# Retention transposes of a gMLP and retention layer moved from TensorE to transposing DMAs, with the scores four steps behind

## What is computed

```python
q = rotary(r_q...); k = rotary(r_k...)            # 128 per head; v has 256 per head
scores = einsum('bnthd,bnshd->bnhts', q, k) * decay     # inside a chunk
inner  = einsum('bnhts,bnshe->bnthe', scores, v)
kv     = einsum('bnshd,bnshe->bnhde', k * w_state, v)   # what a chunk adds to the state
cross  = einsum('bnthd,bnhde->bnthe', q, r_prev) * cross_decay   # r_prev: state before the chunk
ret    = standardize(inner + cross)                     # per head
yb     = (ret * silu(r_z)) @ w_ob
```

## Time and profile before

| | |
|---|---|
| median of 3 runs | 2732.95 us (2732.89 to 2733.12) |
| the profiled execution | 2732.09 us, span 2730.5 us |
| spans of the cores | 2728.6 to 2730.5 us (even), 2684.2 to 2694.5 us (odd) |
| busy on the slowest core (core 2) | PE 2697.4 us (99%), DVE 1108.5 us (41%), ACT 643.5 us (24%) |
| table loads of ACT | 34, 1283 ns each |
| share of the 16 DMA engines | POOL's queue 41.3%, SP's queue 4.6% |

### The profile page before, as it was taken

The page is one execution under the profiler, slowest core; times in us unless marked ns, Lnnn a source line. Parts: engine busy times, 40 slices in busy tenths (PEclk is TensorE's granted clock), DMA queues, the critical chain, the costliest instruction groups (busy, mean ns, idle before and its releaser), DMA issues.

```text
span 2730.5 us, 42159 instructions; the slowest of 8 cores (2684.2 to 2730.5 us)
## 1 busy us (share of the span) xinstructions
PE 2697.4 (99%) x15129; PEld 1420.4 (52%) x15170; DVE 1108.5 (41%) x2686; ACT 643.5 (24%) x1546; POOL 194.5 (7%) x370
## 2 busy tenths in 40 slices
PE   8999999999999999999999999999999999999998
PEld 6556666555555666666544444444555444444443
DVE  1444441166664422222474343411666642122157
ACT  1221110155554111111001211111555621111100
POOL 2000000000000000000001000000000000000000
PEclk9999999999999999999999999999999999999999
DMA  9843444333225433344649464444333544444443
GB/s 159 175 78 63 69 74 71 60 63 58 47 53 109 70 73 68 69 70 70 143 174 214 81 93 72 73 87 76 63 63 63 108 78 89 74 70 86 77 122 134
DMA packets 62420, 241.54 MB, mean 88 GB/s; under 512 B 7424, under 2 KB 7552, under 8 KB 58624
## 3 DMA queue, kind: packets, MB, share of 16 engines
q0 software_dynamic: 52560, 193.49, 41.3%
q1 hardware_dynamic: 9648, 45.27, 4.6%
HBM read 413.31 MB, written 18.87 MB: 158 GB/s over the span
## 4 chain that ended last, share of the span: by engine, by line
PE 97%; DMA 1%; ACT 1%; issue 0%; DVE 0%; POOL 0%; POOLq 0%; DVEq 0%; ACTq 0%
PE ps_all L236 96%; PE ps_all L245 1%; DMA ring<-w 1%; ACT L257 0%; DVE xy_85 L264 0%; ACT aT L257 0%; POOL xT L292 0%; POOL ring L292 0%; POOLq L988 0%; ACT zth_124 L257 0%; DVE stv L282 0%; ACT rs_66 L257 0%; ACT rs_63 L257 0%; ACT rs_65 L257 0%; ACT zth_123 L257 0%
## 5 line engine op out<-in xcount | busy, mean ns | idle before, releaser
L236 PE MATMUL ps_all<-xT,ring 128*128 128x384 bf16 (+1 forms) x6400 | 1206.6, 348 | 0.8 <-ACT rs_65 L257 0.7
L236 PEld LDWEIGHTS ps_all<-xT,ring 128*128 128x128 bf16 x6400 | 622.1, 98 | 536.6 <-issue 2.4
L236 PE MATMUL ps_all<-ring,xT 128*128 128x512 bf16 (+1 forms) x3744 | 731.1, 353 | 5.1 <-DMA xT<-xT 3.1
L236 PEld LDWEIGHTS ps_all<-ring,xT 128*128 128x128 bf16 x3744 | 337.4, 98 | 341.1 <-issue 6.9
L236 PE MATMUL ps_all<-aT,ring 128*128 128x384 bf16 (+1 forms) x2520 | 481.2, 347 | 2.1
L236 PEld LDWEIGHTS ps_all<-aT,ring 128*128 128x128 bf16 x2560 | 250.2, 98 | 220.0
L292 POOL DMA_DIRECT2D ring<-w x352 | 187.7, 541 | 2409.9 <-PE ps_all L236 2013.4
L236 PE MATMUL ps_all<-ring,yT 128*128 128x512 bf16 x1088 | 235.2, 379 | 0.0
L236 PEld LDWEIGHTS ps_all<-ring,yT 128*128 128x128 bf16 x1088 | 106.4, 98 | 128.4
L275 DVE CAST yT<-ps_all 128x384 bf16<-128x384 f32 (+1 forms) x40 | 24.5, 611 | 205.7 <-PE ps_all L236 205.7
L264 DVE SCALAR_TENSOR_TENSOR ogb_129<-ogb_129,ps_all 128x384 f32<-128x384 f32 (+1 forms) x40 | 24.3, 608 | 183.6 <-PE ps_all L236 183.6
(11 more groups left out here) (271 smaller groups left out, 1895.4 us busy)
## 6 DMA issues: line engine op xcount, KB each, us to landing
ring<-w POOLq DMA_DIRECT2D x352, 512.0 KB, 6.3
xy_86<-x SPq DMA_DIRECT2D x9, 1024.0 KB, 6.8
out<-xy_86 SPq DMA_DIRECT2D x18, 512.0 KB, 3.1
xy_85<-x SPq DMA_DIRECT2D x8, 1024.0 KB, 5.4
out<-xy_85 SPq DMA_DIRECT2D x16, 512.0 KB, 2.6
xT<-xT POOLq DMA_DIRECT2D x9, 512.0 KB, 26.3
xT<-xT POOLq DMA_DIRECT2D x4, 1024.0 KB, 21.3
bias_71<-bias_s SPq DMA_DIRECT2D x2, 1024.0 KB, 12.2
```

The source lines that it names most:

```text
L236: return self.S.op("pe", lambda e: e.matmul(out, lhsT=l, rhs=r, start=start, stop=stop), [l, r], [out])
```

## The change

```diff
 def rotary(i):
     ...
+    self.dma_tr("tq%d" % (i % 6), m.qkT[i % 6][:], o[:].rearrange("p j f -> p (j f)"))

 def small_pe(i):
-    a, b_, c_, y = i - 2, i - 3, i - 4, i - 7
-    if 0 <= a < N:
-        for j in range(2):
-            self.tr(self.bank16(3)..., m.qkt[a % 6][:, j, :])
+    b_, c_ = i - 4, i - 5
     ...
-    if 0 <= y < N:
-        for j in range(2):
-            self.tr(self.bank16(7)..., m.ybp[y % 4]...)

 def small_post(i):
     ...
-    if 0 <= a < N:
-        self.act(m.qkT[a % 4]..., self.bank16(3)[:, 0:256], AF.Copy)
     ...
     if 0 <= z < N:          # z = i - 6, before i - 5
         self.act(m.ybp[z % 4][:], self.bank(5 + z % 2)[:, 0:256], AF.Identity, ...)
-    if 0 <= y < N:
-        self.act(self.aT[...], self.bank16(7)..., AF.Copy)
+        self.dma_tr("ty%d" % (z % 4), self.aT[:, 2 * h:2 * h + 2, c * 128:(c + 1) * 128], m.ybp[z % 4][:])
```

The ring is refilled differently during the retention: not four units when a head's last group has been recorded, but one in every other step, behind that step's group:

```diff
-    if c == n - 1:
-        self.w_free()
+    if c % 2 == 0:
+        self.w_issue(self.wpos + NSLOT - 8 + min(4, c // 2 + 1), after=[len(self.S.ops) - 1])
```

The drain has five steps instead of seven, and the first five gate groups wait in banks 0 to 4 until it is over:

```diff
-    drain = i < N + 7
-    b = step % 3 if step < 7 + 3 else self.next_bank()
+    b = i - N if i < N + 5 else self.next_bank()
     self.group(...)
-    if drain:
+    if i < N + 5:
+        held.append((ct, c0, k, b))
         small_pe(i)
         small_post(i)
         i += 1
-    self.act(th, ps, AF.Tanh, scale=0.5)
-    ...
+        if i == N + 5:
+            small_post(i)
+            for g in held:
+                gate(*g)
+    else:
+        gate(ct, c0, k, b)
```

More of the change, by code:

```diff
@@ L292, in load, with w_issue @@
         self.S.op(eng, lambda e: e.dma_start(out=out, in_=in_), list(reads), [out], key=key, after=after)
+    def dma_tr(self, key, out, in_):
+        self.S.op("sp", lambda e: e.dma_start_transpose(out=out, in_=in_), [in_], [out], key=key)
     def store(self, key, out, in_, eng="sp", writes=()):
         self.S.op(eng, lambda e: e.dma_start(out=out, in_=in_), [in_], list(writes), key=key)
-    def w_issue(self, upto):
+    def w_issue(self, upto, after=()):
         ring, w = self.m.ring, self.d["w"]
@@ L301, in w_issue @@
             i = self.wissued
-            self.load("wr%d" % (i % NSLOT), ring[:, i % NSLOT, :, :].rearrange("p k n -> p (k n)"), w[i % NUNIT], "pool")
+            self.load("wr%d" % (i % NSLOT), ring[:, i % NSLOT, :, :].rearrange("p k n -> p (k n)"), w[i % NUNIT], "pool",
+                      after=after)
             self.wissued += 1
@@ L623, in p_mm @@
                         yh_load(h + 1)
-            b = i % 3
+            b = i % 4
             s = slot[h]
             self.group(self.bank(b), [(self.xs(kt, c), m.ring[:, s:s + 4, kt, :]) for kt in range(KT)])
-            if c == n - 1:
-                self.w_free()
+            if c % 2 == 0:
+                self.w_issue(self.wpos + NSLOT - 8 + min(4, c // 2 + 1), after=[len(self.S.ops) - 1])
         def p_post(i):
             h, c = divmod(i, n)
-            b = i % 3
+            b = i % 4
             q32 = m.q32[i % 3]
@@ L660, in small_pe @@
         def small_pe(i):
-            a, b_, c_, y = i - 2, i - 3, i - 4, i - 7
-            if 0 <= a < N:
-                for j in range(2):
-                    self.tr(self.bank16(3)[:, j * 128:(j + 1) * 128], m.qkt[a % 6][:, j, :])
+            b_, c_ = i - 4, i - 5
             if 0 <= c_ < N:
@@ L667, in small_pe @@
                 if not (last and c == n - 1):
-                    self.mm(self.bank(4)[:, 128:384], m.qkt[c_ % 6][:, 1, :], m.v[c_ % 6][:], True, True)
+                    self.mm(self.bank(7)[:, 0:256], m.qkt[c_ % 6][:, 1, :], m.v[c_ % 6][:], True, True)
             if 0 <= b_ < N:
-                self.mm(self.bank(4)[:, 0:128], m.qkT[b_ % 4][:, 1, :], m.qkT[b_ % 4][:, 0, :], True, True)
+                self.mm(self.bank(4)[:, 0:128], m.qkT[b_ % 6][:, 1, :], m.qkT[b_ % 6][:, 0, :], True, True)
             if 0 <= c_ < N:
@@ L673, in small_pe @@
                 self.mm(ob, m.ST[c_ % 3][:], m.v[c_ % 6][:], True, False)
-                self.mm(ob, m.qkT[c_ % 4][:, 0, :], m.Rg[c_ % 3][:], False, True)
-            if 0 <= y < N:
-                for j in range(2):
-                    self.tr(self.bank16(7)[:, j * 128:(j + 1) * 128], m.ybp[y % 4][:, j * 128:(j + 1) * 128])
+                self.mm(ob, m.qkT[c_ % 6][:, 0, :], m.Rg[c_ % 3][:], False, True)
         def small_post(i):
-            a, b_, c_, y = i - 2, i - 3, i - 4, i - 7
-            z = i - 5
+            b_, c_, z = i - 4, i - 5, i - 6
             if 0 <= z < N:
@@ L686, in small_post @@
                 self.stt(r[:, 1:2], mv[:, 0:1], -1.0, r[:, 0:1], ALU.mult, ALU.mult)
-            if 0 <= a < N:
-                self.act(m.qkT[a % 4][:].rearrange("p j t -> p (j t)"), self.bank16(3)[:, 0:256], AF.Copy)
             if 0 <= c_ < N:
@@ L691, in small_post @@
                 if not (last and c == n - 1):
-                    self.stt(m.U[:, h, :], m.U[:, h, :], float(self.gC[h]), self.bank(4)[:, 128:384], ALU.mult, ALU.add)
+                    self.stt(m.U[:, h, :], m.U[:, h, :], float(self.gC[h]), self.bank(7)[:, 0:256], ALU.mult, ALU.add)
             if 0 <= b_ < N:
@@ L702, in small_post @@
             if 0 <= z < N:
+                h, c = divmod(z, n)
                 self.act(m.ybp[z % 4][:], self.bank(5 + z % 2)[:, 0:256], AF.Identity, scale=r[:, 0:1], bias=r[:, 1:2])
-            if 0 <= y < N:
-                h, c = divmod(y, n)
-                self.act(self.aT[:, 2 * h:2 * h + 2, c * 128:(c + 1) * 128],
-                         self.bank16(7)[:, 0:256].rearrange("p (j t) -> p j t", j=2), AF.Copy)
+                self.dma_tr("ty%d" % (z % 4), self.aT[:, 2 * h:2 * h + 2, c * 128:(c + 1) * 128], m.ybp[z % 4][:])
         for i in range(N):
@@ L714, in ret_stage @@
             if c == 1 and init:
-                state_init(h, (i - 1) % 3)
-            if i == 3:
+                state_init(h, (i - 1) % 4)
+            if i == 4:
                 rg_set(0)
@@ L719, in ret_stage, with gate @@
             rotary(i)
+        def gate(ct, c0, k, b):
+            tk = slice(c0 * CH, (c0 + k) * CH)
+            ps = self.bank(b)[:, 0:k * CH]
+            th = m.zth[self.rot("zt", 4)][:, 0:k * CH]
+            self.act(th, ps, AF.Tanh, scale=0.5)
+            self.stt(th, th, 1.0, ps, ALU.add, ALU.mult)
+            a = self.aT[:, ct, tk]
+            self.stt(a, a, 0.5, th, ALU.mult, ALU.mult)
         i = N
-        step = 0
+        held = []
+        self.nbank = 5
         for ct in range(16):
@@ L726, in ret_stage @@
             for (c0, k) in self.sp:
-                tk = slice(c0 * CH, (c0 + k) * CH)
-                drain = i < N + 7
-                b = step % 3 if step < 7 + 3 else self.next_bank()
-                step += 1
-                ps = self.bank(b)[:, 0:k * CH]
-                self.group(ps, [(m.ring[:, s, kt, :], self.xm(kt, c0, k)) for kt in range(KT)])
-                if drain:
+                b = i - N if i < N + 5 else self.next_bank()
+                self.group(self.bank(b)[:, 0:k * CH], [(m.ring[:, s, kt, :], self.xm(kt, c0, k)) for kt in range(KT)])
+                if i < N + 5:
+                    held.append((ct, c0, k, b))
                     small_pe(i)
@@ L736, in ret_stage @@
                     i += 1
-                th = m.zth[self.rot("zt", 4)][:, 0:k * CH]
-                self.act(th, ps, AF.Tanh, scale=0.5)
-                self.stt(th, th, 1.0, ps, ALU.add, ALU.mult)
-                a = self.aT[:, ct, tk]
-                self.stt(a, a, 0.5, th, ALU.mult, ALU.mult)
+                    if i == N + 5:
[4 more added lines that the diff above has]
+                    gate(ct, c0, k, b)
             self.w_free()
@@ L873, in plan_memory @@
     s0 = top[0]
-    top[0] += 32768
+    top[0] += 34816
     assert top[0] <= nc.sbuf_usable_end, (top[0], nc.sbuf_usable_end)
@@ L885, in sub @@
             pos[0] += (size + 31) // 32 * 32
-            assert pos[0] <= s0 + 32768
+            assert pos[0] <= s0 + 34816
             return at(name, shape, dt, off)
@@ L911, in plan_memory @@
     m.v = [a("v%d" % i, [128, 256], BF16) for i in range(6)]
-    m.qkT = [a("qkT%d" % i, [128, 2, 128], BF16) for i in range(4)]
+    m.qkT = [a("qkT%d" % i, [128, 2, 128], BF16) for i in range(6)]
     m.ST = [a("ST%d" % i, [128, 128], BF16) for i in range(3)]
@@ L916, in plan_memory @@
     m.cs = a("cs", [128, NMAX, 128], F32)
-    assert a.pos[0] <= s0 + 24576
-    a = area(24576)
+    assert a.pos[0] <= s0 + 26624
+    a = area(26624)
     m.zth = [a("zth%d" % i, [128, 512], F32) for i in range(4)]
-    a = area(24576)
+    a = area(26624)
     m.yh = [a("yh%d" % i, [128, KT, 128], BF16) for i in range(2)]
```

## The result

The changed kernel took 2708.45, 2708.52 and 2714.13 us, a median of 2708.52 us against 2732.95 us before (executions in which a whole die ran at a lower clock are left out, here and below; with them the medians are 2711.32 and 2733.03 us). The ratio of the means is 0.9917, 95% interval 0.9895 to 0.994. The kernel is faster by 24.4 us at the median (22.6 us by the means), where 38.3 us were forecast. The profiled execution took 2708.52 us, its span is 2706.9 us, and the even cores still decide (2705.4 to 2706.9 us, the odd ones 2675.9 to 2679.5). In the execution of 2714.13 us one core had 2712.5 us; no trace of it was kept, so what it lost is open.

The account below looks back on a forecast made before the run. TensorE's matmul stream on the even cores was taken as the bound. Terms of -29.9 (transposes), -9.9 (drain) and +1.5 us (new waits) sum to -38.3, from 2732.95 to 2694.6 us; own range 2688 to 2702, over all 2686 to 2760.

Parts of the forecast that it names:

- the likeliest case: The forecast itself, all terms summed: 2694.6 us, chance 0.60.
- Step 1, transposes: Retention: transposes leave TensorE, a step goes from 4.06 to 3.84 us, over 136 steps -29.9 us.
- Step 2, the drain: Drain of both tiles: held gates remove 8.5 us of waits and 1.4 us of slow clock, new waits +1.5 us.
- Step 4, ring loads: Ring refill, one load every other step instead of fours at a head's end: nothing, and no loss within 100 us.
- Step 5, latency: Transposing q/k transfers on SP: landing in 6 us against 10.9 us free before the scores, so hidden, cost 0.
- Step 5, rate: Four transfers and one ring load per two steps: 0.98 us each under a 1.19 us limit, SP issue 0.33 us; cost 0.
- C: Rival: q/k transfer lands just too late beside ring loads, 0.15 us a step, +20 us, 2715; chance 0.07.
- D: Rival: transposing transfers can't keep two a step, through short pieces (2907 us) or SP issue of 2.89 us (2958); chance 0.25.

Follow-up runs that it names:

- paced_drain: The changed kernel with no ring load until the drain is over, then two per gate unit: 2693.58 us.
- not_held: paced_drain with each drain group's gate run at once instead of held back: 2711.97 to 2714.21 us.
- y_paced: paced_drain's load pacing, with only the output transposed by DMA and q and k on TensorE, three projection banks, scores three steps behind: 2706.41 to 2706.51 us.
- one_block: paced_drain with each transposing DMA cut in two of one 128x128 block, four a step: 2886.58 and 2889.44 us.
- head_bursts: paced_drain with four ring loads at once at the end of each head except the last, during the retention: 2714.9 us.

## Why the prediction was right, and where it fell short

The direction was right, and the sum of the likeliest case was right for the kernel that the change meant to be: paced_drain has 2693.72 us in its profiled execution, the forecast for it was 2693.8. The agreement to 0.1 us is luck; that to about 2 us is not, as the terms below show. The change itself is 14.7 us behind that, outside the forecast's own range (2688 to 2702 us). It lies inside the range over all only because the rivals had widened that.

- *Step 1, transposes:* right. The step is 3.84 us and stays so: TensorE is busy 251.00 of 251.00 us from 544 to 795 us. From a retention's first group to the first gate group paced_drain is 15.2 and 13.2 us shorter than the kernel before (the latter without the old wait of 0.7 us), 28.4 of the 29.9 us; the last small steps lie behind that point.
- *Step 2, the drain:* right in its terms. The old waits are gone, and the new ones are about those named, 0.6 and 0.4 us in the first drain of paced_drain and 0.7 us in the second, 1.7 us where 1.5 were forecast. That the held gates carry this was said, but its price was not: without them TensorE waits 13.7 us in not_held, more than the 8.5 us before.
- *Step 4, ring loads: this is the step that failed.* It said "Nothing, and no loss within 100 us", and looked only at whether the units come in time for TensorE. The paced refill ends with the last head, and four slots are then given back at once, in the drain. That the loads would collide with the new transfers was not asked at the one place where they are issued together. There they cost 11.8 us of waits for qkT and 4.4 us of slow clock, and paced_drain, which changes only these loads, has neither.
- *Step 5, latency:* the 10.9 us of slack are right in the retention and were carried over to the drain, where the steps are shorter. The late transfer was issued at 808.02, and its scores were next at 815.4: 7.4 us. By paced_drain that alone does no harm, since a transfer without loads beside it is in time. The landing of 6 us was a fair middle of 2.3 to 9.1.
- *Step 5, rate:* the number of packets fits 256-byte rows, as assumed: SP's queue moved 87984 packets over the span instead of 9648, 288 more for each of the 272 transfers, which is 256 and 32 others. From 560 to 795 us, 35424 packets, 123 transfers, took 29.5% of the engines: 0.295 x 235/123 = 0.56 us of all 16 for one, instead of 0.98, and 31 ns a packet. That is the price with two transfers a step among the ring loads. In the first drain of paced_drain, with no load beside them, 2574 packets (8.9 transfers) took 15.0% of 20 us: 0.34 us for one, about the low end of 0.33 that the prediction took from the store. y_paced, with one transfer a step among the ring loads, has 0.33 us (17113 packets, 8.3% of the same 235 us on core 2); what makes the difference was not measured. SP's issue was mis-sized the other way, 1.17 us instead of 0.33, still under the limit of 1.92.
- *The rivals:* what happened is C's mechanism, a q/k transfer late beside ring loads, at 2708 to 2714 us where C had 2715. But C put it into the retention, as a stretch of every step, and it is two waits at the end of the tiles. D is refuted for the change; one_block, with twice as many transfers, shows how near its limb on SP lies.

The Trainium skill (Advanced Engine Details and Errata, section X-Bar Transpose (TRN2)) expects 350 to 400 GB/s of transposing DMAs, from which the prediction estimated 0.16 to 0.19 us for a transfer. The traces have 0.34 us (195 GB/s) with no load beside it and 0.56 us (116 GB/s) with two transfers a step among ring loads; the measurement decides, and either way the sum is the same, as the transfer is hidden in the retention.

## What to carry to other kernels

Here moving work from a full engine to a DMA paid in full only once the DMA's landing time fitted at every place of the loop, also where the loop ends: compare it with the slack there, and look for what else is issued there at once. A prefetch that is harmless for its own reader can still delay a small transfer that someone waits for; pace it with a wait on the consumer's progress, not only on the slot being free. When TensorE stands still for some us, count its slow clock afterwards too: here 4.4 us on top of 11.8.

## What the runs showed of the hardware

- A transposing DMA in SBUF costs SP about 1.2 us whether it turns one 128x128 block (one_block) or two (the changed kernel).
- A transposing transfer of 64 KB took 0.34 us of the engines with no load beside it, and a q/k transfer then landed after 2.4 us. With two a step among loads on POOL's queue it took 0.56 us, with one a step 0.33 us (y_paced). In the changed kernel and in head_bursts a q/k transfer among loads landed after 2.3 to 9.1 us (single loads of 512 KB), 11.2 to 12.7 us (the late ones beside bursts of four) and 14.4 to 15.5 us (the late ones beside four and a fifth). Its own queue did not protect it. How the engines share their time between the two queues was not measured by itself.
- In the last 4 us of a pause of 7 us in TensorE and for some 5 us behind it the granted clock was 0.50 (1.2 GHz), and a group of 16 matmuls of 384 columns took 4.96 us instead of 2.76.
